# An expert-retrieval layer on one core: earlier key scores, U rows twelve places ahead of V rows, diagonals numbered by their own count

## The chip, the cores and the metric

The kernel runs on one core of a Trainium2 chip. It is written engine by engine: TensorE (PE) multiplies, ScalarE (ACT) copies and applies functions, VectorE (DVE) does elementwise work and reductions, GpSimd (POOL) issues the indirect fetches, SyncE (SP) issues the weight loads. Every hand-over is a semaphore. The metric is the device time of one execution in microseconds, as the median of several runs.

## What is computed

Two transformer blocks over 256 tokens of width 1024, all in f32. The first has two attentions, a mixing product and then the PEER layer, which the change touches; the second, over the same tokens and 256 context tokens, has a short convolution layer and a latent attention layer, each with a gated hidden layer. PEER, cut to what matters:

```python
qh = (x_blk @ w_q).reshape(tc, 8, 2, 128)                  # 8 heads, two half queries
scores = einsum('thpc,hpnc->thpn', qh, sub_keys)           # 128 keys each
s_top, i_top = top_k(scores, 16)
cand = s_top[:, :, 0, :, None] + s_top[:, :, 1, None, :]   # 16 x 16 sums
c_s, c_pos = top_k(cand, 16); e_idx = 128 * i_a + i_b      # 16 experts per head
g = softmax(c_s)
a = gelu(einsum('td,thkd->thk', x_blk, expert_u[e_idx]))
out = einsum('thk,thkd->td', g * a, expert_v[e_idx])
```

Every token thus reads 128 rows of the table U and the same 128 rows of V. The output of this block, normed, goes into the second block.

## The kernel before

**The query.** The PEER query is a 1024x2048 product in eight weight chunks of 1 MB (`peer_q` 0 to 7). Each chunk is split: ACT writes a high part (`high`, line 1446), DVE the low part (`low`, line 1791), and TensorE does three products (`product_split`, line 821). Chunks 0 and 1 run together (`first_pair`, line 840). Chunks come through a ring of four slots; a slot is given back when TensorE opens the next chunk (`opens`, line 776), so SP's loads follow TensorE. ACT copies each result out of its PSUM bank (`leave`, line 1416); its loop (line 1573) splits chunk s+3 first and then copies result s. `turn_x2` (line 1065) transposes the normed x for the dots. `peer_scores(g)` (line 1073) multiplies four half queries of tile g//4 with their keys; it needs the two query chunks 2(g%4) and 2(g%4)+1 to have been copied out. Before the change scores 0, 1 and 2 follow chunks 3, 5 and 7, and 3 to 7 stand at the end. The list `PEER` (line 118) numbers these steps, and the number sets which of four banks each uses.

**Choosing.** DVE's `choose(g, at)` (line 2023) finds head g's 16 experts in four steps; the last writes the row indices of 16 places and raises `s_group`. There are 16 groups (8 heads, two token tiles of 128) of 16 places, so 256 places. Group 0's steps are interleaved with the low splits of chunks 5 to 7 (line 2142), group 1 follows, partly between the first dots, and one step of the other groups stands at each fourth place.

**Fetching.** POOL fetches one row per partition, 128x1024 f32, for each place n: a U row into one of six buffers, a V row into one of eight. It first issues U0 to U5 (behind query chunk 5), waits for chunk 7, and then alternates V(n) and U(n+6) (lines 734 to 741). U(n) waits for dot n-6 (line 723), V(n) for the addition of row n-8 (lines 729 and 731). The buffers lie over the split weights and inputs of the query, which is why the first fetches wait for chunks.

**A place.** DVE takes the dot of x with U(n) (line 2155). After four dots ACT applies gelu (line 1606), and DVE weighs them (line 2076), for quad q right after dot 4q+5. Odd places are added by DVE (`add_row`, line 2083) five places after their dot (`ADD_LATER`). For even places ACT makes a 128x128 diagonal matrix of the weights (line 1615), one of eight buffers by n % 8, and TensorE multiplies it with V(n) into a PSUM tile (line 1154). After place 3, `share` needs the exps of groups 0 and 1 (`peer_exp`, line 1584), which ACT does after the last scores copy. After place 127, the first token tile, TensorE adds DVE's sum (line 1167) and ACT copies the tile out in its quad 31 (line 1625), then goes on with gelu 32.

**The context work between.** The second block's work on context tokens is spread over the places by the table `CTX_AT` (line 193): at place n TensorE does one weight chunk after row n; DVE does its share `LATER` = 10 places later (line 2174); ACT copies results in the quad after the place's own (line 1630). Each engine runs its instructions strictly in the order written.

Of the kernel before, what the change touches and what calls it, by code (L numbers as in the profile page):

```python
# [7 lines left out]
P = 128  # L8
# [110 lines left out]
for _s in range(8):  # L119
    PEER.append(("peer_q", _s))  # L120
    if _s == 1:
        PEER += [("turn_x2", _g) for _g in range(2)]
    if _s >= 3 and _s % 2 == 1:
        PEER.append(("peer_scores", _s // 2 - 1))
# [49 lines left out]
UBUFS, VBUFS, DIAGS = 6, 8, 8  # L174
ADD_LATER = 5

# [28 lines left out]
def deep_out(kind, s):  # L205
# [6 lines left out]
    return 8 * (s // 8) + s // 4 % 2 * (cols // WIDE), cols  # L212
LATER = 10
TURN_AT = 131
# [63 lines left out]
def program(nc, w, consts_dram, out_dram):  # L278
    with ExitStack() as ctx:
# [45 lines left out]
        def view(a, at, *dims, dt=None):  # L325
# [5 lines left out]
            else:  # L331
# [41 lines left out]
                 + [std[:, 0, T + P * j:T + P * j + P] for j in range(2)])  # L373
        ubuf = [view(more, D * j, D) for j in (2, 3, 4, 5, 12, 13)]
        vbuf = [view(more, D * j, D) for j in (6, 7, 0, 1, 8, 9, 10, 11)]
# [325 lines left out]
        def _(pool):  # L701
# [31 lines left out]

            wait_full(pool, "peer_q", 5)
            for n in range(UBUFS):
                fetch_u(n)
            wait_full(pool, "peer_q", 7)
            for n in range(SLOTS_P):
                fetch_v(n)
                if n + UBUFS < SLOTS_P:  # L740
                    fetch_u(n + UBUFS)

# [15 lines left out]
        def _(pe):  # L758
# [325 lines left out]
            first_pair("peer_q", 1)  # L1084
            turn_x2()
            for s in range(2, 8):
                product_split("peer_q", 0, s)
                if s >= 3 and s % 2 == 1:
                    peer_scores(s // 2 - 1)
# [57 lines left out]
            for n in range(SLOTS_P):  # L1147
                if n == P:
                    pe.wait_ge(s_ptok, 2)
                if by_tensor(n):  # L1150
                    pe.wait_ge(s_diag, rows_by(by_tensor, n + 1))
                    pe.wait_ge(v_landed[n % VBUFS], 16 * (n // VBUFS + 1))
                    for c in range(2):
                        mm = nc.tensor.matmul(vo[:, 512 * c:512 * c + 512], diags[n % DIAGS],  # L1154
                                              vbuf[n % VBUFS][:, 512 * c:512 * c + 512],
                                              start=(n % P == 0), stop=False)
                    mm.then_inc(s_vdone, 1)
# [234 lines left out]
        def _(act):  # L1392
# [180 lines left out]
            for s in range(8):  # L1573
# [3 lines left out]
                if s == 1:  # L1577
                    leave_x2()
                if s >= 3 and s % 2 == 1:
                    scores(s // 2 - 1)  # L1580
# [22 lines left out]
            for quad in range(SLOTS_P // 4):  # L1603
# [6 lines left out]
                for n in range(4 * quad, 4 * quad + 4):  # L1610
                    if by_vector(n):
                        continue
                    if n >= DIAGS:
                        act.wait_ge(s_vdone, rows_by(by_tensor, n - DIAGS + 1))
                    nc.scalar.activation(diags[n % DIAGS], ident, ACT.Copy, scale=wts[:, n % 16:n % 16 + 1])\  # L1615
                        .then_inc(s_diag, 1)
# [5 lines left out]
                if quad == SLOTS_P // 4 - 1:  # L1622
                    prepare_root()
                    high("conv_in_lat", 2)
                if quad % (P // 4) == P // 4 - 1:
                    for c in range(2):
                        act.wait_ge(s_vsum, 2 * (quad // (P // 4)) + c + 1)
                        here = slice(512 * c, 512 * c + 512)
# [123 lines left out]
        def _(v):  # L1752
# [266 lines left out]
            norm_split(1, "norm2", lambda k: vcol("norm2", k))  # L2019
            for s in range(3, 5):  # L2020
                low("peer_q", s)

# [119 lines left out]
            for at in range(4):  # L2142
                choose(0, at)
                if at < 3:
                    low("peer_q", 5 + at)
            choose(1, 0)
            to_choose = [(g, at) for g in range(2, GROUPS_P) for at in range(4)]
            v.wait_ge(s_xtile, 1)
            wait_emptied(v, "turn_x2", 1)
            for n in range(SLOTS_P):  # L2150
# [10 lines left out]
                if n % 4 == 3:  # L2161
# [5 lines left out]
                    if n // 4 < len(to_choose):  # L2167
                        choose(*to_choose[n // 4])
                if n == TURN_AT + LATER:
                    add_first_tile()  # L2170
                    final_gains()
# [169 lines left out]
```

## Time and profile before

| | |
|---|---|
| median of 3 runs | 1984.39 us (1984.15 to 1986.63) |
| the profiled execution's own time | 1963.2 us |
| its span | 1961.4 us |
| mean granted TensorE clock | 0.946 |
| busy: TensorE, DVE, ACT, POOL | 87%, 63%, 31%, 31% |
| HBM read | 513.53 MB, 262 GB/s over the span |
| chain that ended last, by engine | PE 49%, DMA 21%, DVE 17%, POOL 5%, issue 5%, ACT 3% |
| first and last POOL fetch issued | 370.2 and 1174.5 us |

The profile is of one execution; its times are from the start of the span. Busy shares are means over stages with different limits, so a stage has to be read by itself. A row of an engine in order of time gives the start, the length, the instruction, and in brackets the idle time before it with what ended it. Lines are those of the kernel.

### The profile page before, as it was taken

The numbers are of one execution on the slowest core, as the hardware profiler recorded it, in microseconds if no ns is written. First come the engines' busy times: TensorE is split into PE (matmuls) and PEld (weight loads), VectorE is DVE, ScalarE is ACT, GpSimd is POOL, SyncE is SP. The second block draws the span as 40 slices with busy tenths as digits, with TensorE's granted clock in tenths as the row PEclk, the third lists the DMA queues.
The fourth block names the chain that finished last, engine by engine and source line by source line (L and its number), as shares of the span: only waits on it lengthen the run. The fifth ranks groups of instructions, "written<-read, shape, count | busy, mean of one in ns | idle before, by whom it ended". The sixth has DMA issues, their size and how long they took to land.

```text
span 1961.4 us, 26217 instructions
## 1 busy us (share of the span) xinstructions
PE 1697.7 (87%) x10406; PEld 1346.7 (69%) x10406; DVE 1229.4 (63%) x2125; ACT 604.3 (31%) x907; POOL 608.2 (31%) x570
## 2 busy tenths in 40 slices
PE   6999999798838578798868868989999887889998
PEld 5887679765616255475536547979999644569998
DVE  4334236787797996878787666555543279635552
ACT  4346534311111112121211113334532122635532
POOL 1111100377657676576767760000000100000000
PEclk9999889999979789898989999999999999999999
DMA  8999854799989999999999993536653222025553
GB/s 279 310 303 317 278 198 160 256 407 409 409 323 407 390 386 409 361 406 408 408 409 409 409 398 128 183 96 193 190 178 128 78 61 88 1 86 180 185 193 107
DMA packets 222960, 515.99 MB, mean 263 GB/s; under 512 B 13244, under 2 KB 121996, under 8 KB 222860
## 3 DMA queue, kind: packets, MB, share of 16 engines
q0 software_dynamic: 86784, 318.80, 42.4%
q1 hardware_dynamic: 135728, 195.71, 29.6%
q8 instruction: 66, 1.08, 0.2%
q14 instruction: 34, 0.28, 0.0%
q10 hardware_dynamic: 348, 0.11, 0.0%
HBM read 513.53 MB, written 1.05 MB: 262 GB/s over the span
## 4 chain that ended last, share of the span: by engine, by line
PE 49%; DMA 21%; DVE 17%; POOL 5%; issue 5%; ACT 3%; ACTq 0%; DVEq 0%; SPq 0%; POOLq 0%
DMA more<-in_peer_v_dram,idx 16%; PE bank L816 10%; PE bank L819 10%; PE bank L817 9%; POOL more L715 5%; PE bank L770 4%; DVE more L2155 4%; DMA more<-in_peer_u_dram,idx 3%; DVE nrm L2095 2%; PE bank L923 2%; DVE rstd L2226 2%; PE bank L1044 2%; PE wide L1154 1%; PE bank L1105 1%; PE wide L931 1%
## 5 line engine op out<-in xcount | busy, mean ns | idle before, releaser
L1769 DVE TENSOR_TENSOR low_weights<-weights,high_weights 128x2048 fp32r<-128x2048 f32 x108 | 247.4, 2292 | 305.1 <-ACT high_weights L1450 304.4
L816 PE MATMUL bank<-high_input,high_weights 128*128 128x256 f32 x1312 | 374.1, 285 | 17.3 <-DVE low_input L1818 8.2
L2155 DVE CUSTOM_DVE_ANT_0 more<-more,wide 128x1024 f32<-128x1024 f32 x256 | 311.7, 1218 | 121.2 <-DMA more<-in_peer_u_dram,idx 119.4
L817 PE MATMUL bank<-high_input,low_weights 128*128 128x256 f32 x1344 | 378.7, 282 | 0.0
L715 POOL DMA_INDIRECT more<-in_peer_u_dram,idx x256 | 294.2, 1149 | 269.4 <-DVE dots L2155 114.8
L819 PE MATMUL bank<-low_input,high_weights 128*128 128x256 f32 x1312 | 371.6, 283 | 0.0
L1154 PE MATMUL wide<-more,rstd 128*128 128x512 f32 x384 | 214.0, 694 | 157.6 <-ACT rstd L1615 138.2
L1450 ACT ACTIVATE high_weights<-weights 128x2048 fp32r<-128x2048 f32 x108 | 206.8, 1915 | 310.9 <-DMA weights<-in_ffn_w_gate_dram 92.5
L715 POOL DMA_INDIRECT more<-in_peer_v_dram,idx x256 | 260.2, 1016 | 90.0 <-issue 74.1
L816 PEld LDWEIGHTS bank<-high_input,high_weights 128*128 128x128 f32 x1312 | 249.2, 190 | 20.6 <-issue 18.0
L1154 PEld LDWEIGHTS wide<-more,rstd 128*128 128x128 f32 x384 | 79.0, 215 | 263.0 <-ACT rstd L1615 158.8
L817 PEld LDWEIGHTS bank<-high_input,low_weights 128*128 128x128 f32 x1344 | 258.9, 193 | 0.0
L1105 PE MATMUL bank<-nrm,weights 128*128 128x256 f32 x1088 | 249.5, 388 | 10.1 <-DVE big L1769 6.3
L1105 PEld LDWEIGHTS bank<-nrm,weights 128*128 128x128 f32 x1088 | 214.0, 197 | 60.6 <-issue 27.9
L819 PEld LDWEIGHTS bank<-low_input,high_weights 128*128 128x128 f32 x1312 | 249.4, 190 | 0.0
L2095 DVE SCALAR_TENSOR_TENSOR nrm<-more,wts,nrm 128x1024 f32<-128x1024 f32 x126 | 162.3, 1288 | 28.0 <-issue 23.4
L1615 ACT ACTIVATE rstd<-consts,wts 128x128 f32<-128x128 f32 x96 | 35.0, 396 | 418.4 <-DVE wts L1769 418.4
L747 POOL MEMSET big<- 32x1024 f32 x4 | 3.8, 944 | 325.6 <-PE bank L819 325.4
L819 PE MATMUL bank<-low_hidden,high_weights 128*128 (+1 forms) x352 | 99.0, 281 | 0.0
L816 PE MATMUL bank<-high_hidden,high_weights 128*128 (+1 forms) x352 | 98.8, 281 | 0.0
L817 PE MATMUL bank<-high_hidden,low_weights 128*128 (+1 forms) x352 | 98.3, 279 | 0.0
L1606 ACT ACTIVATE gelus<-dots 128x4 f32<-128x4 f32 x64 | 13.1, 205 | 233.7 <-DVE dots L2155 233.6
(250 smaller groups left out, 2400.2 us busy)
## 6 DMA issues: line engine op xcount, KB each, us to landing
weights<-in_ffn_w_down_dram SPq DMA_DIRECT2D x33, 1024.0 KB, 4.9
weights<-in_ffn_w_gate_dram SPq DMA_DIRECT2D x30, 1024.0 KB, 5.4
weights<-in_ffn_w_up_dram SPq DMA_DIRECT2D x30, 1024.0 KB, 5.3
weights<-in_conv_w_in_dram SPq DMA_DIRECT2D x24, 1024.0 KB, 8.3
weights<-in_w_in_dram SPq DMA_DIRECT2D x20, 1024.0 KB, 9.4
nrm<-in_mod_w_dram POOLq DMA_DIRECT2D x16, 1024.0 KB, 7.8
sq<-in_mod_w_dram POOLq DMA_DIRECT2D x16, 1024.0 KB, 7.1
h_ctx<-in_mod_w_dram POOLq DMA_DIRECT2D x16, 1024.0 KB, 7.3
```

The source lines that it names most:

```text
L715: nc.gpsimd.indirect_dma_start(out=dst, out_offset=None, in_=w[table][0], in_offset=at)\
L770: mm = nc.tensor.matmul(b[:, m * width:(m + 1) * width], wt[:, k, m * P:(m + 1) * P], rhs(k), start=(k == 0), stop=(k == kt - 1))
L816: first = nc.tensor.matmul(out, cut(high), hi, start=start, stop=False, **more_args)
L817: nc.tensor.matmul(out, cut(w_lo[b]), hi, start=False, stop=False, **more_args)
L819: return first, nc.tensor.matmul(out, cut(high), lo, start=False, stop=stop, **more_args)
L923: mm = nc.tensor.matmul(bank[bank_of("mods", j)][rows, 0:WIDE], cvec[:, k, :], mod_w[j % 3][:, k, :], start=(k < 4), stop=(k >= 4))
L1105: mm = nc.tensor.matmul(bank[b][:, (m % 2) * T:(m % 2) * T + T], wt[:, k, m * P:(m + 1) * P], rhs(2 * (s % 4) + k), start=(s % 4 == k == m ...
L1154: mm = nc.tensor.matmul(vo[:, 512 * c:512 * c + 512], diags[n % DIAGS], vbuf[n % VBUFS][:, 512 * c:512 * c + 512], start=(n % P == 0), sto ...
L1450: nc.scalar.activation(high_of(stage, s)[:, :], ring[b][:, :], ACT.Copy).then_inc(w_high[b], 1)
L1769: return nc.vector.tensor_tensor(out, a, b, op)
L2095: done = nc.vector.scalar_tensor_tensor(vsum, row, wt, vsum, ALU.mult, ALU.add)
L2155: nc.vector.tensor_tensor_reduce(u, u, wide[0][:, :], 1.0, 0.0, ALU.mult, ALU.add, dots[:, n % 16:n % 16 + 1]).then_inc(s_dot, 1)
```

## The change

The key scores of group 0 move from behind query chunk 3 to behind the transposes after chunks 0 and 1, scores 1 and 2 from behind chunks 5 and 7 to behind 4 and 6, on TensorE, ACT and in the list of banks. DVE takes the low splits of chunks 4 to 7 later: 4 after step 1 of group 0, 5 and 6 after step 3, 7 after the first step of group 1. POOL issues twelve U rows first (U2 waits for chunk 4, U4 for chunk 5), then waits for chunk 7 and alternates V(n) and U(n+12); the buffers remain six and eight, with the two that overlap nothing of the query first. DVE adds its rows eleven places after their dot, and its context work comes 16 places later instead of 10 (the first tile's addition 12 places after place 131 instead of 10). The diagonals are numbered by the count of TensorE's rows, so that the eight buffers span sixteen places. ACT copies the first tile out in quad 33 instead of 31.

```diff
@@ -119,8 +119,8 @@
     if _s == 1:
-        PEER += [("turn_x2", _g) for _g in range(2)]
-    if _s >= 3 and _s % 2 == 1:
+        PEER += [("turn_x2", _g) for _g in range(2)] + [("peer_scores", 0)]
+    if _s in (4, 6):
         PEER.append(("peer_scores", _s // 2 - 1))
@@ -172,7 +172,9 @@
 UBUFS, VBUFS, DIAGS = 6, 8, 8
-ADD_LATER = 5
+U_AHEAD = 12
+SUM_AT = [P // 4 + 1, SLOTS_P // 4 - 1]
+ADD_LATER = 11
 
@@ -210,7 +212,7 @@
     return 8 * (s // 8) + s // 4 % 2 * (cols // WIDE), cols
-LATER = 10
+LATER = 16
 TURN_AT = 131
@@ -371,7 +373,7 @@
                  + [std[:, 0, T + P * j:T + P * j + P] for j in range(2)])
-        ubuf = [view(more, D * j, D) for j in (2, 3, 4, 5, 12, 13)]
+        ubuf = [view(more, D * j, D) for j in (12, 13, 2, 3, 4, 5)]
         vbuf = [view(more, D * j, D) for j in (6, 7, 0, 1, 8, 9, 10, 11)]
@@ -731,14 +733,15 @@
 
-            wait_full(pool, "peer_q", 5)
-            for n in range(UBUFS):
+            for n in range(U_AHEAD):
+                if n in (2, 4):
+                    wait_full(pool, "peer_q", 4 + n // 4)
                 fetch_u(n)
...
                 fetch_v(n)
-                if n + UBUFS < SLOTS_P:
-                    fetch_u(n + UBUFS)
+                if n + U_AHEAD < SLOTS_P:
+                    fetch_u(n + U_AHEAD)
 
@@ -1083,9 +1086,10 @@
             turn_x2()
+            peer_scores(0)
             for s in range(2, 8):
                 product_split("peer_q", 0, s)
-                if s >= 3 and s % 2 == 1:
+                if s in (4, 6):
                     peer_scores(s // 2 - 1)
@@ -1151,7 +1155,7 @@
                     for c in range(2):
-                        mm = nc.tensor.matmul(vo[:, 512 * c:512 * c + 512], diags[n % DIAGS],
+                        mm = nc.tensor.matmul(vo[:, 512 * c:512 * c + 512], diags[rows_by(by_tensor, n) % DIAGS],
                                               vbuf[n % VBUFS][:, 512 * c:512 * c + 512],
@@ -1576,7 +1580,8 @@
                     leave_x2()
-                if s >= 3 and s % 2 == 1:
+                    scores(0)
+                if s in (4, 6):
                     scores(s // 2 - 1)
@@ -1610,9 +1615,10 @@
                         continue
-                    if n >= DIAGS:
-                        act.wait_ge(s_vdone, rows_by(by_tensor, n - DIAGS + 1))
-                    nc.scalar.activation(diags[n % DIAGS], ident, ACT.Copy, scale=wts[:, n % 16:n % 16 + 1])\
+                    m = rows_by(by_tensor, n)
+                    if m >= DIAGS:
+                        act.wait_ge(s_vdone, m - DIAGS + 1)
+                    nc.scalar.activation(diags[m % DIAGS], ident, ACT.Copy, scale=wts[:, n % 16:n % 16 + 1])\
                         .then_inc(s_diag, 1)
@@ -1622,9 +1628,9 @@
                     high("conv_in_lat", 2)
-                if quad % (P // 4) == P // 4 - 1:
+                if quad in SUM_AT:
                     for c in range(2):
-                        act.wait_ge(s_vsum, 2 * (quad // (P // 4)) + c + 1)
+                        act.wait_ge(s_vsum, 2 * SUM_AT.index(quad) + c + 1)
                         here = slice(512 * c, 512 * c + 512)
@@ -2017,8 +2023,7 @@
             norm_split(1, "norm2", lambda k: vcol("norm2", k))
-            for s in range(3, 5):
-                low("peer_q", s)
+            low("peer_q", 3)
 
@@ -2141,9 +2146,11 @@
                 choose(0, at)
-                if at < 3:
-                    low("peer_q", 5 + at)
+                if at % 2 == 1:
+                    low("peer_q", 4 + at // 2)
+            low("peer_q", 6)
             choose(1, 0)
+            low("peer_q", 7)
             to_choose = [(g, at) for g in range(2, GROUPS_P) for at in range(4)]
@@ -2166,7 +2173,7 @@
                         choose(*to_choose[n // 4])
-                if n == TURN_AT + LATER:
+                if n == TURN_AT + 12:
                     add_first_tile()
```

## Rows read from the trace of the kernel before

**Rows 1.** the page, 40 slices of 49 us: what DMA moved

```profile
GB/s 279 310 303 317 278 198 160 256 407 409 409 323 407 390 386 409 361 406 408 408 409 409 409 398 128 183 96 193 190 178 128 78 61 88 1 86 180 185 193 107
```

**Rows 2.** stretches: length, PE PEld DVE ACT POOL busy, clock, DMA share, GB/s

```profile
370.00:375.00 5.00, 5.00 (x45) 5.00 (x44) 2.20 (x14) 0.60 (x1) 3.87 (x4) 1.00 0.56 191
560.00:600.00 40.00, 25.32 (x60) 13.46 (x61) 39.16 (x87) 6.27 (x15) 27.18 (x25) 0.74 0.85 301
640.00:720.00 80.00, 48.22 (x133) 27.43 (x132) 78.56 (x169) 10.92 (x27) 55.49 (x51) 0.80 1.00 383
800.00:840.00 40.00, 29.80 (x94) 19.99 (x95) 38.64 (x95) 6.05 (x15) 23.90 (x23) 0.83 0.91 346
```

**Rows 3.** who waited for whom, 371 to 1177 us: us, times, longest

```profile
DVE more L2155 <- DMA more<-in_peer_u_dram,idx: 119.4, 88, 3.5
...
PE wide L1154 <- ACT rstd L1615: 131.3, 31, 13.2
...
POOL more L715 <- PE wide L1154: 13.2, 11, 7.2
```

**Rows 4.** ACT in order of time: start, us, instruction, idle before it

```profile
341.95 1.92 ACT L1450 ACTIVATE high_weights<-weights 128x2048 fp32r<-128x2048 f32 x1 [5.01 <-DMA weights<-in_peer_w_q_dram]
343.77 1.55 ACT L1424 ACTIVATE big<-bank 128x512 f32<-128x512 f32 x3
...
376.70 0.60 ACT L1424 ACTIVATE big<-bank 128x512 f32<-128x512 f32 x1 [5.06 <-PE bank L819]
...
382.12 0.60 ACT L1424 ACTIVATE more<-bank 128x512 f32<-128x512 f32 x1 [0.30 <-PE bank L1079]
...
385.28 0.22 ACT L1586 ACTIVATE gates_p<-gates_p 128x16 f32<-128x16 f32 x1 [0.94 <-DVE gates_p L1769]
```

**Rows 5.** DVE in order of time, same columns

```profile
353.32 0.49 DVE L2029 MAX8 top_scratch<-more 128x8 f32<-128x128 f32 x2 [7.13 <-ACT more L1424]
...
369.18 0.17 DVE L2059 CAST idx<-top_scratch 128x16 uint32<-128x16 f32 x1
...
386.30 0.16 DVE L2072 RECIPROCAL top_scratch<-top_scratch 128x1 f32<-128x1 f32 x1
...
390.11 1.22 DVE L2155 CUSTOM_DVE_ANT_0 more<-more,wide 128x1024 f32<-128x1024 f32 x1
```

**Rows 6.** TensorE: the x2 turns, and the clock after an idle stretch

```profile
L1068 PE MATMUL wide<-consts,nrm x8: 272/272/273, 336.8 to 337.6; 128*128 128x128 f32 x8
...
1201.95 0.55 PE L816 MATMUL bank<-high_input,early_high_weights 128*128 128x256 f32 x1 [4.09 <-DVE low_input L1818]
...
1201.90:1205.20 3.30, 3.25 (x15) 3.29 (x16) 3.30 (x9) 2.03 (x4) 0.00 (x0) 0.51 0.39 104
```

**Rows 7.** POOL's fetches in order of time, and their landing over the stage

```profile
370.22 1.03 POOL L715 DMA_INDIRECT more<-in_peer_u_dram,idx  x1 [106.84 <-DVE idx L2059]
...
395.48 0.94 POOL L715 DMA_INDIRECT more<-in_peer_v_dram,idx  x1 [0.30 <-issue]
...
DMA to landing us min/median/max: 4.3/15.1/19.9
```

**Rows 8.** the tile boundary: ACT, DVE and POOL in order of time

```profile
796.38 0.60 ACT L1629 ACTIVATE big<-wide 128x512 f32<-128x512 f32 x1 [16.82 <-PE wide L1167]
...
799.39 0.16 DVE L1769 TENSOR_TENSOR wts<-gelus,gates_p 128x4 f32<-128x4 f32 x1 [7.90 <-ACT gelus L1606]
...
831.08 1.15 POOL L715 DMA_INDIRECT more<-in_peer_v_dram,idx  x1 [7.20 <-PE wide L1154]
```

**Rows 9.** an up chunk: ACT's copies and table load, TensorE's chunk

```profile
740.37 2.06 ACT L1424 ACTIVATE big<-bank 128x512 f32<-128x512 f32 x4
742.45 1.28 ACT L1606 ACT_TABLE_LOAD   x1
...
832.36 7.07 PE L1105 MATMUL bank<-nrm,weights 128*128 128x256 f32 x32
```

**Rows 10.** the last V fetch on POOL

```profile
1174.52 2.74 POOL L715 DMA_INDIRECT more<-in_peer_v_dram,idx  x1 [2.08 <-DVE nrm L2095]
```

## The prediction

> **What bounds it now.** I read the page first: from 370 to 1182 us the DMA engines move 406 to 409 GB/s in most of the slices [rows 1]. That is the retrieval stage, 512 row fetches of 128x1024 f32 (524,288 bytes, so 1.28 us each at 409 GB/s) and the context weights. The stage is therefore priced in DMA time: a stretch below 409 is lost, work moved inside a full stretch is free. The table by stretches shows the losses [rows 2]: 301 GB/s in 560:600 (108/409 of 40 us, 10.6 us), 383 in 640:720 (5.1 us), 346 in 800:840 (6.2 us). DVE is busy for 39.2 of 40 and 78.6 of 80 us in the first two: the convolutions, the residual and the context norm lie there on top of the dots, and DVE's work is the limit. The waits say the same: DVE waits 119.4 us for U rows over the stage, POOL only 13.2 us for TensorE's rows [rows 3], 7.2 us of it in one wait at 831 [rows 8]. For the start I read each engine in order of time [rows 4 to 7].
>
> **Start, TensorE.** The change puts the first key scores right after the two turned x tiles. They need query chunk 1 out of its bank. ACT reaches that copy only after splitting weight chunk 4, for which it waits 5.01 us on a DMA; split at 341.95, the copy is the first of the three at 343.77 and ends at about 344.4 [rows 4]. TensorE ends the last x2 turns at about 338.8 (336.8 plus sixteen transposes, eight in a microsecond [rows 6]). Today it goes on with chunk 2 at once; after the change it is held for 5.6 us, with every later query chunk queued behind. After an idle 4.09 us elsewhere the granted clock of the next 3.3 us was 0.51, the lower level, at twice the spacing [rows 6]; I add 1.5 us. So: 344.4 + 1.0 (scores) + 6 chunks of 5.66 us (ACT's idle 5.06 plus its copy 0.60 at 376.70 [rows 4]) + 2 scores of 0.9 + 1.5 = 382.7 for the end of chunk 7, against 376.5 now.
>
> **Start, ACT and the dots.** The last key scores follow chunk 7. Today six are left (copies until 382.72), then five: 382.7 + 0.6 + 0.3 + 5x0.9 = 388.1. Behind them on ACT stand a table load of 1.28 us and the two exps, whose second ends 2.9 us after the copies today (385.28 + 0.3) but only because it waits 0.94 us for DVE [rows 4]; 2 us without that. DVE's share of group 0, after dot 3, waits for the exps: about 390.2. Today DVE gets there at 386.30 without a wait and ends dot 4 5.0 us later, at 391.33 [rows 5]. After the change dot 4 ends at 395.2.
>
> **Start, POOL.** Group 0's indices come sooner. Today choose 0 runs from 353.32 to 369.35 with three low splits of 2.2 us inside, so 9.4 us alone [rows 5]. From the new scores (copied at 346.3) with one split inside it ends at 357.9, and the first U fetch goes at 358.7, not 370.22 [rows 7]: 11.5 us of head start. But U rows have six buffers before and after. U0 to U5 go as chunks 4 and 5 free the space, U6 to U9 each need one of dots 0 to 3, and U10 needs dot 4, at 395.2. V0, which now stands behind U11, goes at about 398. Ten U rows have landed by 395.5; POOL today has issued 19 fetches by then, from the first row of [rows 7] to the second, seven of them V rows. In DMA time: today 191 GB/s over 370:375 [rows 2] and 409 over the next 20.5 us is 9.3 MB, less one weight chunk of 1.05 MB (128x2048 f32) 8.2 MB, or 15.7 fetches. The change is 5.7 fetches behind, 7.3 us, and must fill an empty queue again at 395, as at 370:375, where (409-191)/409 of 5 us is 2.7 us. **Start: +10 us.** Bounds: +4, DVE's own lag (395.2 less 391.3), if the queue is full sooner than I think; +14 if weight chunk 7 lands late behind U rows and holds low(7) and the dots too.
>
> The Trainium skill, DMA: Bandwidth & Descriptors, Specifications, gives about 358 GB/s of HBM per core; a fetch would cost 1.46 us by it and the 5.7 fetches 8.3 us. The rows disagree, slices of 49 us stand at 409 GB/s [rows 1], and I keep the row.
>
> **Middle, steady state.** V rows are issued right behind U(n+11) instead of U(n+5), and added 11 places after their dot instead of 5. Issue to use stays six places, a V buffer is held as long, and fetches in flight stay at most 6 + 8. With 15.1 us from issue to landing [rows 7] and 3.2 us a place (1.28x2 plus a quarter of a 1 MB chunk) a V row lands at about dot n+10. What changes is TensorE: it waits no more for diagonals (a place n row needs dot n+5 or so) but only for the row. Where the DMA is full this is worth nothing. The two stretches bound by DVE keep all their instructions, six places later on: 0, bounds -2 and +3. The diagonals over sixteen places are eight buffers as before, with no more instructions.
>
> **Middle, tile boundary.** Today ACT is held in quad 31 for 16.82 us until TensorE has added the vector sum; gelu 32 stands behind, DVE waits 7.90 us for it, and a backlog ends in POOL's 7.20 us wait [rows 8]. Now the copy is at quad 33, add 127 comes at place 138 and gelu 34 is wanted at 141, three places for the chain instead of one: DVE waits some 3 us. TensorE's rows have two places of slack to their buffer's next use. I give back 5 of the 6.2 us lost in 800:840 [rows 2]; bounds 0 and -6.2.
>
> **Middle, new waits.** ACT's place does not move, TensorE's does, from about dot n+5 to n+10. At up chunk 3 (place 110) the copies are due in quad 28, and gelu 29 behind them is wanted at dot 121. V110 lands at dot 120, then a row of 1.8 us, the chunk of 7.07 us, four copies of 2.06 us and a table load of 1.28 us [rows 9]: 12.2 us, less one place of 3.2, a DVE wait of about 9 us. By the same count 1.6 us at each of the three conv_in copies, 3 at the context norm and 3 at up chunk 11. DVE has 119 us of waiting to pay from [rows 3], and the queue holds 14 fetches, 18 us. Only where DVE is the limit does it cost: +2; bounds 0 and +8.
>
> **Tail.** Twelve V rows now follow the last U row, not six. They are in the DMA count above. The last V fetch waits 2.08 us for a DVE add today [rows 10]; the adds now follow the residual too. -1; bounds -3 and +2.
>
> **Sum:** 10 - 5 + 2 - 1 = +6 us on the profiled execution's own 1963.2 us (span 1961.4): 1969.2. The median of the three runs is 1984.39, 21 us more; I have no row for that difference and add the change to it unscaled: 1990.4 us.
>
> **Rivals.**
> Faster: the boundary pays and the start hardly costs. The place is V0's issue: if the exps are reached by about 385, dot 4 stays at 391 and V0 comes at 393, the fetches owed are three instead of six (+4); with the whole 6.2 us at the boundary and 3 in the tail it is -5, 1979. For it: the first indices are 11.5 us sooner, and TensorE waits 131.3 us for diagonals [rows 3] that now are early. Against: DVE's order puts share before dot 4. It decides below a start cost of 6 us.
> Nothing to measure: start and boundary cancel, within 4 us. Six U buffers make "twelve ahead" an order of issue, not more rows under way, so that the change does not do what it says is part of this. 1984 to 1988.
> Much slower: the 9 us DVE wait at dot 121 and those at 101 and 157 meet a short queue, since POOL stands on one U fetch with the V fetches behind. Then 8 us are lost there, +12 to +14, 1998.
>
> **Chances.** Forecast (+3 to +10) 0.42; faster rival 0.22; cancelling 0.22; much slower 0.14. The range goes from 1978 (the faster rival's end) to 1999. 0.2% is 4 us, about what a measurement of this kernel tells from none: faster 0.23, same 0.26, slower 0.51.
>
> **What would show it.** TensorE idle from about 339 to 344 before the first key scores; the first U fetch near 359, the first V fetch near 398, a DVE wait of near 8 us on the exps after dot 3; GB/s low until 395; no long POOL wait on TensorE after the boundary; a DVE wait on gelu some 30 us ahead of it; and the last V fetch, now at 1174.5 [rows 10], near 1180. I am wrong if V0 is issued before 390, or if the two DVE-bound stretches lose clearly less than 15.7 us.

## The result and the profile after

The changed kernel took 1986.14 us (median of 20 runs, 1978.58 to 1990.66) and the kernel before 1980.68 us (20 runs, 1975.11 to 1988.43): ratio 1.0027, 95% interval 1.0016 to 1.0038. It is slower by 5.5 us. The profiled execution of it took 1985.16 us, with a span of 1983.4 us. One execution of the kernel before (7389.49 us) and two of ahead_only below (2055.70 and 2762.92 us) were far slower than all others, and ratios leave them out.

Its page reads like [rows 1], with other holes. DMA, 40 slices of 49.6 us:

```profile
GB/s 267 310 303 317 285 177 148 233 348 409 409 375 356 407 307 394 409 388 408 408 409 409 409 399 131 212 108 189 182 181 148 77 49 98 1 85 170 190 189 109
```

The slice of 307, from 694 us, is new; the 361 of [rows 1] at the tile boundary is shallower, 388. To compare executions whose clocks start differently I count from ACT's split of weight chunk 4 (341.95 in [rows 4], 346.10 here) and call that instant t0. The stage's end is DVE's first reciprocal after the last add. It comes 875.1 us after t0 here, 856.5 in the profile of before.

Who waited for whom in the profile after, from 363 to 1205 us (total, times, longest):

```profile
PE wide L1158 <- DMA more<-in_peer_v_dram,idx: 115.2, 40, 15.7
...
ACT big L1428 <- PE bank L1109: 72.6, 17, 15.2
...
DVE wts L1775 <- ACT gelus L1611: 45.6, 7, 12.7
...
DVE more L2162 <- DMA more<-in_peer_u_dram,idx: 41.9, 38, 2.2
...
POOL more L717 <- PE wide L1158: 11.5, 8, 2.7
...
PE wide L1158 <- ACT rstd L1621: 3.1, 1, 3.1
```

TensorE no longer waits for diagonals (131.3 us in [rows 3], 3.1 here). It waits for V rows. ACT, whose place did not move, waits for the chunks that TensorE now reaches later, and DVE waits for the gelus queued behind ACT's copies. DVE's waiting for U rows, its reserve, fell from 119.4 us to 41.9. POOL's long wait on TensorE (7.20 us in [rows 8]) is gone.

The start. The four engines' own timelines in the profile after, with the columns of [rows 4]: TensorE's first key scores, ACT's copies of chunk 7 and of the last scores, DVE's choose 0 and its share of group 0, POOL's first U fetch and U10.

```profile
348.54 2.07 PE L1082 MATMUL bank<-big 128*128 128x128 f32 x8 [5.63 <-ACT big L1428]
```
```profile
387.61 0.60 ACT L1428 ACTIVATE big<-bank 128x512 f32<-128x512 f32 x1 [5.00 <-PE bank L822]
...
393.03 0.60 ACT L1428 ACTIVATE more<-bank 128x512 f32<-128x512 f32 x1 [0.30 <-PE bank L1082]
```
```profile
351.28 0.49 DVE L2034 MAX8 top_scratch<-more 128x8 f32<-128x128 f32 x2 [11.31 <-ACT more L1428]
...
395.28 0.16 DVE L2077 RECIPROCAL top_scratch<-top_scratch 128x1 f32<-128x1 f32 x1 [10.69 <-ACT gates_p L1591]
```
```profile
363.19 2.90 POOL L717 DMA_INDIRECT more<-in_peer_u_dram,idx  x1 [98.83 <-DVE idx L2064]
...
400.58 0.94 POOL L717 DMA_INDIRECT more<-in_peer_u_dram,idx  x1 [14.79 <-DVE dots L2162]
```

Put on the old time base (less 4.15 us), the first U fetch is at 359.0, U10 at 396.4 and V0 at 398.9. Before V0 the queue runs dry, and from 393 to 398 nothing moves at all:

```profile
388.00:393.00 5.00, 4.73 (x40) 4.54 (x40) 0.00 (x0) 2.60 (x5) 0.00 (x0) 1.00 0.68 270
393.00:398.00 5.00, 0.00 (x0) 0.00 (x0) 2.51 (x15) 3.88 (x8) 0.00 (x0) 0.96 0.00 0
```

The middle, first TensorE's timeline, then ACT's and then DVE's in the profile after. "Remote" means that the profile shows no instruction for the event that ended the wait:

```profile
694.66 3.62 PE L803 MATMUL bank<-sq,consts 128*128 128x256 f32 x16
...
827.28 1.88 PE L1171 MATMUL wide<-nrm,consts 128*128 128x512 f32 x4
```
```profile
705.44 0.47 ACT L1428 ACTIVATE std<-bank,consts 128x256 f32<-128x256 f32 x1 [14.32 <-remote]
...
772.73 0.60 ACT L1428 ACTIVATE big<-bank 128x512 f32<-128x512 f32 x1 [14.97 <-PE bank L1109]
```
```profile
707.47 0.16 DVE L1775 TENSOR_TENSOR wts<-gelus,gates_p 128x4 f32<-128x4 f32 x1 [7.69 <-ACT gelus L1611]
...
777.46 0.16 DVE L1775 TENSOR_TENSOR wts<-gelus,gates_p 128x4 f32<-128x4 f32 x1 [12.73 <-ACT gelus L1611]
...
834.92 0.75 DVE L2097 TENSOR_SCALAR nrm<-more,wts 128x1024 f32<-128x1024 f32 x1 [9.50 <-remote]
```

These are the context norm (dot 101), the up copies (dot 121) and the tile boundary. TensorE's first row is the sums that the norm's copy at 705.44 needs, its second the addition of DVE's sum that the boundary needs: they end at 698.28 and 829.16, and ACT goes on 7 and 5 us later, DVE 6 us after the second. What that is comes below.

Five stretches of the stage in the profile after, from t0 to t0+100, then +200 to +300, +300 to +350, +350 to +400 and +400 to +550 (columns as [rows 2]):

```profile
346.10:446.10 100.00, 76.78 (x460) 66.56 (x461) 75.20 (x201) 27.35 (x46) 44.70 (x43) 0.86 0.76 287
546.10:646.10 100.00, 65.28 (x178) 36.35 (x177) 88.41 (x199) 14.53 (x34) 63.16 (x60) 0.85 0.96 366
646.10:696.10 50.00, 36.52 (x99) 19.84 (x99) 41.36 (x91) 6.26 (x15) 36.20 (x35) 0.89 1.02 407
696.10:746.10 50.00, 32.70 (x97) 20.43 (x96) 41.62 (x82) 7.99 (x18) 28.93 (x28) 0.80 0.84 309
746.10:896.10 150.00, 130.21 (x454) 89.51 (x453) 112.48 (x263) 27.99 (x58) 95.58 (x93) 0.93 1.01 397
```

and in the first profile of before, the first and the fourth of them:

```profile
341.90:441.90 100.00, 85.06 (x498) 71.20 (x497) 77.21 (x200) 29.42 (x50) 53.09 (x52) 0.95 0.87 332
...
692.00:742.00 50.00, 44.15 (x163) 31.51 (x164) 43.45 (x99) 10.08 (x23) 36.98 (x35) 0.92 1.00 386
```

A stretch loses its length times (409 less its GB/s) over 409. So after loses 29.8 us in the first 100 us where before lost 18.8, and 12.2 us around the context norm where before lost 2.8. In all, the stage is 18.6 us longer in the profile, and the timed runs say 5.5. The first experiments had to settle this.

### The profile page after: what moved, and what is told of

The parts are those of the page before. It is cut to its first block and busy times, and to the rows that moved or that the text cites. A ratio compares the mean times of both kernels' runs of the same rounds, so it can differ in the third digit from the quotient of the medians.

```text
span 1983.4 us, 26214 instructions
## 1 busy us (share of the span) xinstructions
PE 1723.4 (87%) x10406; PEld 1358.9 (69%) x10406; DVE 1225.4 (62%) x2125; ACT 605.8 (31%) x907; POOL 596.7 (30%) x570
## 5 line engine op out<-in xcount | busy, mean ns | idle before, releaser
L717 POOL DMA_INDIRECT more<-in_peer_u_dram,idx x256 | 284.7, 1112 | 283.1 <-DVE dots L2162 115.9
L2162 DVE CUSTOM_DVE_ANT_0 more<-more,wide 128x1024 f32<-128x1024 f32 x256 | 310.9, 1216 | 74.3 <-DMA more<-in_peer_u_dram,idx 41.9
L1158 PE MATMUL wide<-more,rstd 128*128 128x512 f32 x384 | 220.4, 708 | 122.5 <-DMA more<-in_peer_v_dram,idx 97.9
L1109 PE MATMUL bank<-nrm,weights 128*128 128x256 f32 x1088 | 262.6, 400 | 18.9 <-issue 11.7
L1109 PEld LDWEIGHTS bank<-nrm,weights 128*128 128x128 f32 x1088 | 220.6, 203 | 77.5 <-issue 41.9
L1428 ACT ACTIVATE big<-bank 128x512 f32<-128x512 f32 (+1 forms) x98 | 56.9, 590 | 151.3 <-PE bank L1109 72.6
```

What stands on the lines that cost most here:

```text
L717: nc.gpsimd.indirect_dma_start(out=dst, out_offset=None, in_=w[table][0], in_offset=at)\
L1109: mm = nc.tensor.matmul(bank[b][:, (m % 2) * T:(m % 2) * T + T], wt[:, k, m * P:(m + 1) * P], rhs(2 * (s % 4) + k), start=(s % 4 == k == m ...
L1158: mm = nc.tensor.matmul(vo[:, 512 * c:512 * c + 512], diags[rows_by(by_tensor, n) % DIAGS], vbuf[n % VBUFS][:, 512 * c:512 * c + 512], sta ...
L1428: nc.scalar.activation(dst, src, func, scale=scale, **more_args).then_inc(free[b], 1)
L2162: nc.vector.tensor_tensor_reduce(u, u, wide[0][:, :], 1.0, 0.0, ALU.mult, ALU.add, dots[:, n % 16:n % 16 + 1]).then_inc(s_dot, 1)
```

## First experiments: which part, and how far two profiles of one kernel differ

These four ran on one chip, called the first below. **after_again** is the kernel after unchanged, **before_again** the kernel before.

> The changed kernel unaltered, timed again beside the one before. Expected 1.0027 times the time before, +5 us, as in the first comparison. Its profile is wanted as a second one: in the first, the retrieval stage grew by some 18 us against the profile before, while the medians differ by 5.5 us. If the start and the copies on ACT explain the medians, the second profile again shows TensorE held 5 to 6 us before the first key scores, DVE waiting 10 to 11 us for the exps, and the first V fetch 20 to 21 us later than before relative to the query's start; the rest of the 18 us should not recur.

> The kernel before, for a second profile of it. The first had a time of its own of 1963.2 us, under every one of the other twenty runs (1975.1 to 1988.4). Expected near 1980 us, with the missing 15 us or so lying in the retrieval stage as lower GB/s. If the profile is again near 1963, the profiled execution is simply faster and the two profiles can be compared as they stand.

after_again: 1986.74 us (12 runs), ratio 1.0025 (1.0001 to 1.0048); stage 875.3 us in its profile, with 29.6 us lost in the first 100 and 12.5 around the context norm, the same as after within half a microsecond. So what was expected not to come again, came again. before_again: 1987.96 us in its one run, stage 872.7 us, 16 us longer than in the first profile of the same kernel.

**scores_only** keeps the new order of the key scores and puts the fetch order, add times, sum copy and final gains back:

```diff
-U_AHEAD = 12
-SUM_AT = [P // 4 + 1, SLOTS_P // 4 - 1]
-ADD_LATER = 11
+U_AHEAD = 6
+SUM_AT = [P // 4 - 1, SLOTS_P // 4 - 1]
+ADD_LATER = 5
-LATER = 16
+LATER = 10
```

> Only the start of the change: key scores after the x2 turns and the low splits moved; U rows six ahead, additions 5 and context work 10 places later, tile copied in quad 31, all as before. Theory A (the start sets the loss: TensorE held 5.6 us and DVE held on the exps while no V row may go): TensorE and the exps are as late as in the changed kernel, but V0 to V4 now go from about 4 us after 383 on, so 15 fetches are out by 395 instead of 19 before and 10 after: +4 to +6 us on the kernel before. Rival B (the loss lies in the middle, where ACT's copies wait for TensorE's later chunks, and the start costs nothing): within 2 us of the kernel before.

**ahead_only** is the opposite: the old order of the key scores on all engines, with the new numbers kept.

> Only the fetch order and what goes with it: U rows twelve ahead, additions 11 and context work 16 places later, tile copied in quad 33, diagonals over sixteen places; key scores and low splits in their old places. Theory A: V0 stands behind U11, which needs dot 5, so it goes at about 394 instead of 378 and 12 fetches are out where 18 were: about 7 us lost at the start, 4 to 5 gained at the tile boundary, 2 lost in the middle: +3 to +7 us. Rival B: +5 us or more, all of it in the middle, with the start at most +2.

scores_only: 1978.95 us, ratio 0.9991 (0.9971 to 1.001). ahead_only: 1984.31 us (the median of the ten runs that its ratio rests on), ratio 1.0026 (1.0005 to 1.0046). The whole loss goes with the twelve places. The new places of the scores alone cost nothing that can be measured, though DVE waited 11.4 us for the exps in scores_only's profile and V0 went at t0+41.2, not t0+35.9. Which part of the stage the loss comes from, the two times can't tell: +5 us is in the range of both expectations for ahead_only. Its profile has losses in both parts, 30.3 us in the first 100 us, with V0 at t0+56.6, and 13.0 around the context norm.

## Taking the new waits away one at a time

**exps_early**: the kernel after, with ACT's first two exps ahead of the last key scores' copies.

```diff
                 if s in (4, 6):
                     scores(s // 2 - 1)
+                if s == 6:
+                    peer_exp(0)
+                    peer_exp(1)
             for g in range(3, 8):
                 scores(g)
...
-            peer_exp(0)
-            peer_exp(1)
             for quad in
```

> The kernel after, with ACT's first two exps put after its copies at query chunk 6, ahead of the last key scores' copies. In the profile after, DVE waits 10.7 us for them at 395.28 before its share of group 0 and before dot 4, POOL waits 14.8 us for dot 4, and V0 goes at 403.07; the queue moves nothing from about 393 to 401. Theory A, the start carries the loss: DVE's wait is gone, dot 4 ends some 9 us sooner, V0 is issued at about 393 or 394 on that time base (47 us after ACT's split of weight chunk 4, not 57), and 6 to 9 us less are lost in the first 100 us: 1978 us. Rival B, the middle carries it: V0 moves as much, but the time stays within 2 us of the kernel after, 1985 to 1988, as scores_only had the same DVE wait (11.4 us) and lost nothing by it.

**act_later**: ACT's context copies come one quad, four places, later.

```diff
-                for n in range(4 * quad - 4, 4 * quad if quad < SLOTS_P // 4 - 1 else SLOTS_P):
+                for n in range(4 * quad - 8, 4 * quad - 4 if quad < SLOTS_P // 4 - 1 else SLOTS_P):
```

> The kernel after, with ACT's copies of the context part put one quad (four places) later. In the profile after, ACT stands 14.3 us at the context norm and 15.0 us at an up copy until TensorE has done chunks that are now six places later, DVE waits 7.7 and 12.7 us for the gelu behind them, and 12 us of DMA time are missing in the 40 us after the first of them. Rival B, these waits carry the loss: DVE's waits for gelus fall from 45.6 us to under 15, the 50 us stretch that lost 12 to 13 us loses under 5, and the time is 1977 to 1980. Theory A, the start carries it: the waits fall as well, but the rows lost there come back elsewhere or were hidden, and the time is within 2 us of the kernel after, 1985 to 1988.

**all_three** adds to these two the scores behind chunk 2 (the edit of chunk2_first, below).

> The kernel after with three edits: first key scores behind query chunk 2 (TensorE does not stand 5.6 us for ACT's copy of chunk 1), the first two exps early (as exps_early), ACT's context copies a quad later (as act_later). If both stretches carry the loss and add up: 8 from the start, 8 from the middle, 2 to 4 from TensorE's hold, 1968 us. If the time is set elsewhere (a DVE sum that cannot shrink, other losses that grow), 1976 or more.

**scores_only_mended** is scores_only with chunk2_first's and exps_early's edits.

> The kernel before with the key scores' new places, first scores behind query chunk 2, and the two exps early; lookahead, adds and diagonals as before. scores_only took 1978.95 us with a DVE wait of 11.4 us on the exps. Theory A, the start counts: with that wait gone and V0 at about 36 us after ACT's split of weight chunk 4 rather than 41, 5 to 9 us less: 1971 to 1974, faster than both kernels. Rival B, the start is covered by rows that would wait later: 1977 to 1981.

These four ran on a second chip, where the kernel before takes 1967.47 us (35 runs, 1960.86 to 1974.52), 13 us less than on the first. So ratios are compared, or kernels on this chip with each other.

| kernel | us | ratio | 95% interval | stage in its profile |
|---|---|---|---|---|
| exps_early | 1969.61 | 1.0008 | 0.9999 to 1.0018 | 857.8 |
| act_later | 1970.76 | 1.0017 | 1.0004 to 1.003 | 862.4 |
| all_three | 1965.16 | 0.9984 | 0.9969 to 0.9998 | 851.7 |
| scores_only_mended | 1970.97 | 1.0016 | 1.0003 to 1.0029 | 862.5 |

exps_early did as theory A said for the start: no wait of DVE for the exps, V0 at t0+45.6, and 22.0 us lost in the first 100 instead of 29.8. In time it did half of what was expected: 8 us less than after were forecast, and its ratio is 0.0019 below after's 1.0027, or 4 us. Its first stretch and the one around the context norm:

```profile
348.10:448.10 100.00, 83.83 (x485) 69.97 (x486) 79.73 (x211) 27.47 (x46) 52.23 (x50) 0.92 0.86 319
...
698.10:748.10 50.00, 39.90 (x128) 24.95 (x128) 48.69 (x114) 7.75 (x17) 33.68 (x34) 0.86 0.96 366
```

act_later did as rival B said for the middle. Its waits from 340 to 1215 us, and its last two stretches:

```profile
DVE more L2162 <- DMA more<-in_peer_u_dram,idx: 108.1, 93, 3.1
...
DVE wts L1775 <- ACT gelus L1611: 0.3, 1, 0.3
```
```profile
700.40:750.40 50.00, 36.55 (x123) 22.82 (x122) 49.21 (x109) 10.20 (x21) 36.07 (x36) 0.93 1.00 386
750.40:900.40 150.00, 127.31 (x464) 88.77 (x463) 118.34 (x264) 30.40 (x61) 102.93 (x95) 0.97 1.03 409
```

DVE's waits for gelus are down to 0.3 us, and its reserve is back at 108.1. The 50 us around the context norm lose 2.8 us and the 150 us after them nothing, where after lost 12.2 and 4.4. Here too the time fell short: 1977 to 1980 us was expected, and a ratio of 1.0017 is 1984 us on the first chip, hardly below after's.

These 12.2 us are not the right thing to compare with, though. exps_early has after's context copies, and on this chip its profile reads, from TensorE's sums for the norm to DVE's waits at dots 101, 121 and the boundary:

```profile
689.20 3.62 PE L803 MATMUL bank<-sq,consts 128*128 128x256 f32 x16
```
```profile
692.85 0.47 ACT L1428 ACTIVATE std<-bank,consts 128x256 f32<-128x256 f32 x1 [7.19 <-PE bank L803]
```
```profile
694.87 0.16 DVE L1776 TENSOR_TENSOR wts<-gelus,gates_p 128x4 f32<-128x4 f32 x1 [2.51 <-ACT gelus L1612]
...
765.46 0.16 DVE L1776 TENSOR_TENSOR wts<-gelus,gates_p 128x4 f32<-128x4 f32 x1 [14.20 <-ACT gelus L1612]
...
816.92 0.75 DVE L2098 TENSOR_SCALAR nrm<-more,wts 128x1024 f32<-128x1024 f32 x1 [3.38 <-PE wide L1171]
```
```profile
DVE wts L1776 <- ACT gelus L1612: 47.6, 9, 14.2
```

ACT's copy starts 0.03 us after the end of TensorE's sums, not 7.2 us after it as in after, and DVE waits 2.5 us for the gelu at the context norm, not 7.7. The stretch loses 5.3 us with the same copies. So most of after's 12.2 us there go with the late start of one copy, which exps_early's edit does not touch. On the second chip the later copies are worth 47.6 us of DVE's waits against 0.3, and in DMA time 5.3 less 2.8 and 1.8 less 0.

all_three shows the gains together:

```profile
350.20:450.20 100.00, 81.42 (x470) 68.28 (x469) 80.25 (x214) 28.29 (x50) 53.20 (x51) 0.93 0.85 321
...
700.20:750.20 50.00, 40.77 (x130) 26.07 (x131) 47.22 (x106) 8.45 (x19) 36.81 (x37) 0.86 1.01 394
750.20:900.20 150.00, 129.32 (x471) 89.72 (x470) 119.70 (x267) 29.97 (x61) 105.16 (x96) 0.97 1.03 409
```

In timed runs of that one chip: all_three is 4.5 us below exps_early, which is the copies (and chunk 2), and 5.6 us below act_later, which is the exps (and chunk 2). So both waits are real. If the two gains add up, the kernel after would take 1969.61 + 1970.76 - 1965.16 = 1975.2 us there, an estimate, 7.7 over before, a ratio of 1.0039; its three comparisons elsewhere gave 1.0027, 1.0025 and 1.0036. On this chip it did not run. Neither theory was enough alone. The expectation for all_three was too large: 1968 us was meant for a chip where before takes 1980, so 12 us less than before, and it was 2.3 less. scores_only_mended missed as well, it is 3.5 us above before. Against it, all_three has the twelve places and the later copies, and is 5.8 us faster.

## The hold on TensorE, and a third profile of before

These four ran on a third chip, where the kernel before takes 1980.48 us (29 runs).

**chunk2_first**: the kernel after with the first key scores one query chunk later, on TensorE and in ACT's copies.

```diff
             turn_x2()
-            peer_scores(0)
             for s in range(2, 8):
                 product_split("peer_q", 0, s)
+                if s == 2:
+                    peer_scores(0)
```

ACT's copy and the list of the order follow.

> The kernel after, with the first key scores behind query chunk 2 on TensorE and ACT's copy of them to match: TensorE does not stand 5.6 us for ACT's copy of chunk 1. If that hold moves the end, every later query chunk comes 3 to 6 us sooner, the exps too, and DVE's 10.7 us wait for them shrinks by as much: ratio to the kernel before 1.0005 to 1.001, 3 to 4 us less than after. This is what all_three (0.9984) leaves over once exps_early and act_later (4 us and 2 us less than after) are added up. If weight chunk 4 and its splits set TensorE's pace anyway, the hold only moves and the ratio stays within 0.0005 of after's, 1.0020 to 1.0032.

> The kernel after, unchanged, on the chip of this call, for the sum of the parts. Ratio 1.0020 to 1.0033 if it carries over between chips; the profiled stage 875 us long from ACT's split of weight chunk 4, as in both profiles so far, with 8 us lost in the second 50 us and 12 in the 50 us of the context norm.

> The kernel before with the key scores' new places alone, once more, since scores_only (0.9991) and scores_only_mended (1.0016) disagree and ran on different chips. If the start does not set the end under the old order of fetches, it is 0.998 to 1.001 again. If the first value was a lucky one and the start costs what theory A said, it is 1.002 to 1.003.

> A third profile of the kernel before. The first had a span of 1961.4 us and a stage of 856.5 us, the second 1986.2 and 872.7, and the timed runs lie between or above. If the second is the usual case, this one again shows 870 or more, with 9 us lost in the second 50 us; if the first is, 857 with none.

after_third (the kernel after): 1987.12 us, ratio 1.0036 (1.002 to 1.0052), stage 873.3. chunk2_first: 1984.65 us, ratio 1.002 (1.0007 to 1.0033), stage 873.1; the intervals overlap, so the time leaves open whether 2.5 us are real. scores_only_again (scores_only unchanged): 1979.39 us, ratio 0.999 (0.9978 to 1.0002), as the first time, so the first value was not luck. The trace of chunk2_first shows where TensorE's hold went:

```profile
351.05 1.13 PE L1084 MATMUL bank<-big 128*128 128x128 f32 x8 [0.20 <-ACT big L1431]
362.30 0.58 PE L821 MATMUL bank<-high_input,high_weights 128*128 128x256 f32 x1 [4.46 <-DVE low_weights L1779]
```

The 5.6 us before the scores are gone, and 4.5 us before a later query chunk have come, for DVE's low split of its weights, which stands behind choose 0. ACT copies chunk 7 at t0+41.1, at t0+41.5 in after, and V0 goes at t0+56.5 against 57.0. The hold was real and cost next to nothing: without it, DVE's split holds TensorE nearly as long.

before_third is the kernel before. Its one run took 1983.43 us, its stage 868.6. Its timelines at the last key scores: ACT's copies, then TensorE's score products, which end at 394.4, then DVE's share of group 0:

```profile
388.99 0.60 ACT L1424 ACTIVATE big<-bank 128x512 f32<-128x512 f32 x1 [7.21 <-remote]
...
394.17 0.60 ACT L1424 ACTIVATE more<-bank 128x512 f32<-128x512 f32 x1 [1.85 <-issue]
399.15 0.60 ACT L1424 ACTIVATE more<-bank 128x512 f32<-128x512 f32 x1 [4.39 <-issue]
402.03 0.60 ACT L1424 ACTIVATE more<-bank 128x512 f32<-128x512 f32 x1 [2.28 <-remote]
```
```profile
389.64 4.73 PE L1079 MATMUL bank<-big 128*128 128x128 f32 x40 [1.95 <-ACT big L1424]
```
```profile
404.28 0.16 DVE L2072 RECIPROCAL top_scratch<-top_scratch 128x1 f32<-128x1 f32 x1 [7.88 <-ACT gates_p L1586]
```

In the first profile these copies follow each other every 0.9 us, up to 382.12 [rows 4]. Here and in before_again they are strung out over 13 us, and DVE waits 7.9 and 8.1 us for the exps behind them. So two of the three profiles of before already had the wait that I charged to the change.

The traces also keep the semaphore events, the signals by which one engine releases another, and these say whose delay it is. The last score product ends at 394.37, the signal that its bank is full is recorded at 402.01, and ACT's copy starts at 402.03. In before_again the same signal comes 6.1 us after the product's end. ACT is not late, its signal is. At after's context norm the signal comes at 705.42, 7.1 us after the sums' end, and at its tile boundary 5.6 us after. (The ends of matmuls in a profile are modelled, so the product itself may be what is late.) I counted the copies and additions of ACT and DVE in the stage that start on a signal of TensorE's recorded over 1 us late. They come in two kinds of profile:

| profiles | late signals in the stage | lateness, us | semaphore events recorded |
|---|---|---|---|
| first of before; the four of the second chip | none | | 15,507 to 15,509 |
| the nine others (first and third chip, and after) | 2 to 10 each | 1.3 to 10.6 | 11,387 to 12,302 |

The nine also lack a fifth to over a quarter of the events. Late signals are not of one kernel: with the old order of the scores they strike chunk 7's or the scores' copies (before_again, before_third, ahead_only), and with the twelve places the context norm (after three times, chunk2_first, ahead_only). exps_early, act_later and all_three, on the second chip, have none there. So a profile of one kind must not be held against one of the other.

The first two stretches of interest of before_third, t0 to t0+100 and t0+350 to +400:

```profile
352.00:452.00 100.00, 79.47 (x474) 67.56 (x474) 71.11 (x191) 26.55 (x44) 45.60 (x46) 0.91 0.79 297
...
702.00:752.00 50.00, 34.19 (x121) 24.18 (x122) 42.17 (x85) 8.23 (x18) 33.63 (x31) 0.80 0.92 347
```

DMA time lost, each from its stretch as above:

| stretch after t0 | before, first | before_again, _third | after, _again, _third | ahead_only | scores_only, _again | exps_early | act_later | all_three |
|---|---|---|---|---|---|---|---|---|
| 0 to 100 | 18.8 | 27.6, 27.4 | 29.8, 29.6, 29.1 | 30.3 | 23.5, 23.0 | 22.0 | 30.1 | 21.5 |
| 200 to 300 | 10.5 | 10.5, 9.8 | 10.5, 10.8, 10.5 | 10.8 | 10.8, 11.2 | 10.8 | 10.3 | 10.0 |
| 300 to 350 | 2.2 | 3.5, 1.0 | 0.2, 0.2, 0.0 | 0.0 | 4.3, 1.1 | 0.2 | 0.0 | 0.7 |
| 350 to 400 | 2.8 | 7.0, 7.6 | 12.2, 12.5, 11.4 | 13.0 | 2.0, 7.8 | 5.3 | 2.8 | 1.8 |
| 400 to 550 | 6.2 | 6.2, 5.9 | 4.4, 4.0, 4.0 | 8.1 | 6.2, 6.6 | 1.8 | 0.0 | 0.0 |
| stage | 856.5 | 872.7, 868.6 | 875.1, 875.3, 873.3 | 878.4 | 865.0, 868.8 | 857.8 | 862.4 | 851.7 |

In each column the stage is the sum of its five losses plus 816 to 819 us, so the five account for the stage, whatever caused them.

The first profile's 1963.2 us lies below every timed run of before on the first and third chip (from 1971.83 us up) and inside the range of the second. Like that chip's profiles it has no late signal. It looks like an execution of the kind that chip gives. No profile of before was taken there, so this is argued, not shown. It would also explain scores_only_mended: its first stretch loses 22.5 us, 3.7 more than 18.8, and it is 3.5 us slower.

## Why the prediction was right, and where its sum was not

**The size.** I forecast +6 us and measured +5.5, with the forecast as the likeliest of the four cases. The time itself, 1986.14 us, is 4.3 below the 1990.4 that I named, because the median of three runs that I started from, 1984.39, became 1980.68 with twenty. By the time alone it lies in the range of the rival in which all cancels (1984 to 1988), by the difference in the forecast's.

**The sum, like with like.** The prediction stood on one profile without late signals. Its counterpart would be a profile of after without them, and there is none. But act_later has after's start, and exps_early has its middle, both on the second chip. Put together as an estimate, against the first profile of before: start +11.3 us (30.1 less 18.8), the stretch to 350 -2.0, the context norm +2.5, the 150 us with the boundary -4.4, 200 to 300 +0.3. That is +7.7, and the timed runs of that chip add up to 7.7 as well. Forecast were start +10, DVE-bound stretches 0, new waits +2, boundary -5, tail -1. So each of the first four is within 2 us; the tail this can't tell. (exps_early's queue fills sooner, which may help its middle too.)

On the other chips the pieces differ. Against before_again and before_third, the three profiles of after give, in the mean: start +2.0, 200 to 300 +0.5, to 350 -2.1, the context norm +4.7, the 150 us behind it -1.9. That is +3.2, and the stages differ by 3.9. But both sides hold late signals, at different places (after's 7 us are in the +4.7), and outside the stage the same executions differ by 6 us the other way: by their whole times (1987.96 and 1983.43; 1985.16, 1981.58 and 1984.69) after would be the faster. So these profiles can't price the terms. On these chips the agreement of the total is in part luck.

**Start, TensorE**: right in itself (5.6 us forecast, 5.63 measured; chunk 7 copied at 383.5 on the old time base, 382.7 forecast for its end), wrong as a cause. chunk2_first removed the hold and chunk 7 came 0.4 us sooner. What I left out was DVE: choose 0, now earlier, stands ahead of the low splits that the query chunks need.

**Start, ACT and the dots; POOL**: each step as forecast. First U fetch 359.0 (358.7), DVE's share 391.1 (390.2), V0 398.9 (about 398). The start loses 11.0 us more than in the first profile (+10 forecast). "Today DVE gets there at 386.30 without a wait" holds for one of three profiles of before. In the other two DVE waits about 8 us there, behind a signal that is 6 to 8 us late, and against them the term is +2. exps_early shows that the wait is worth removing: 8.1 us of DMA time against act_later on the same chip, and 4 to 6 us of time (by its ratio against after's, and by act_later against all_three, which has chunk 2 as well).

**Steady state and the DVE-bound stretches**: 0 forecast; the stretch from 200 to 300 lost 10.5 to 10.8 us in after and 9.8 to 10.5 in before, and the one to 350 lost 2 us less than before. Within the bounds, and the sign that would have proved me wrong did not come. That TensorE would wait for rows alone and no more for diagonals is what the waits show.

**Tile boundary**: the gain was right, the wait was another. In exps_early the stretch gave back 4.4 us of the 5 forecast, and DVE waited 3.4 us of the 3 forecast. But it did not wait for gelu 34, which was ready. It waited with its first addition for the second tile (place 129, after dot 140): `add_row` may overwrite the sum only when TensorE has added it, and the last addition of the first tile comes after dot 138. In after the signal for that was 5.6 us late, DVE waited 9.5 us, and the stretch gave back 1.8.

**New waits on ACT**: the mechanism and the places were right. At dot 121 "about 9 us" was 12.7, and 14.2 in exps_early. The queue was full, and POOL's next stretch lost 1 or 2 us. At up chunk 11 "3" was 8.6, and 5.6 in exps_early. At the context norm "3" was 2.5 in exps_early, and 7.7 in after, where the signal is 7.1 us late. Behind it DMA moved 166 GB/s over ten microseconds, and 12 us were lost in all. The "much slower" rival said that such a wait would meet a short queue. One did, at dot 101, but with a late signal that the rival did not have, and at 4.7 us of its 8.

**Tail**: -1 forecast. The five stretches leave about +1 to it, which is within their errors. The last V fetch was to go 6 us later and goes 11 us later against before_again and before_third (t0+857.1, 857.0 and 855.5, against 847.2 and 843.1), and the end follows it by 18 us rather than 25.

**The faster rival** had its case in the wrong place. The boundary and the context copies could pay, but only with ACT moved along with TensorE: all_three is 2.3 us faster than before (0.9984, 0.9969 to 0.9998), the lowest ratio of all, though scores_only's 0.9991 and 0.999 can't be told from it.

What stays open: what makes the signals late and why on two chips only, and whether the missing events belong to it; and how after compares with before on the second chip, where neither was profiled and after was not run.

## What to carry to other kernels

When one engine's share of a pipeline moves by six places, look at every engine that consumes its results in a hand-written order, or the wait only changes its owner. Moving ACT's copies by four places was enough to end DVE's waits for them (47.6 us to 0.3), and with two more small edits the change went from 0.3% slower to 0.2% faster. A held engine is only a cost if nothing else would hold it as long: look for the next producer it needs before charging the wait. And take two or three profiles of the kernel before: if the profiled run lies far from the median, 21 us here, find what differs before adding a sum to it. A profile from another chip is no baseline either: exps_early showed a loss at the context norm shrink from 12.2 to 5.3 us that its edit does not touch.

## What was not expected of the hardware

Two profiles of one kernel differed by 16 us in a stage of 860. 9 us of it arose in the first 100 us, where ACT's 0.6 us copies came up to 5 us apart and TensorE's signals were recorded up to 7.6 us after the modelled end of its products (before_third, 394.37 and 402.01). Such signals, up to 10.6 us late, stand in all nine profiles of this kind and in none of the five others. The kernel after has one at the same place each time (7.1, 7.2 and 6.6 us late at the context norm) and repeated its stage within 2 us over three profiles. The same kernel before took 1980.2, 1967.5 and 1980.5 us as median on the three chips, with the DMA at 409 GB/s in full slices on each. The slower two are the ones with late signals; whether these are the whole difference is open.
